# Two attention stages of a decoder step put into one fixed order of 328 ticks

## What is computed

```python
def stick_breaking_block(q, k, v, bias, q_pos, k_pos):
    z = jnp.einsum('bqhd,bkhd->bhqk', q.astype(jnp.float32), k.astype(jnp.float32)) * (HEAD_DIM ** -0.5)
    z = z + bias.astype(jnp.float32)[None, :, None, None]
    causal = k_pos[None, :] < q_pos[:, None]
    log_1m_beta = jnp.where(causal, jax.nn.log_sigmoid(-z), 0.0)
    tail = lax.cumsum(log_1m_beta, axis=3, reverse=True) - log_1m_beta
    w = jnp.where(causal, jnp.exp(jax.nn.log_sigmoid(z) + tail), 0.0)
    return jnp.einsum('bhqk,bkhd->bqhd', w.astype(v.dtype), v)
...
            k_past = cache_k[l][page_table].reshape(n_seq_s, past_len, N_HEADS_A, HEAD_DIM)
            v_past = cache_v[l][page_table].reshape(n_seq_s, past_len, N_HEADS_A, HEAD_DIM)
```

## Time and profile before

| | |
|---|---|
| median of 3 runs | 3228.53 us (3222.68 to 3229.23) |
| profiled execution, time / span | 3214.24 us / 3212.8 us |
| granted TensorE clock, mean | 0.942 of 2.4 GHz |
| prompt attention | from 728.4 us on |
| sample attention | from 1295.8 us on |
| router phase | from 1736.3 us on |

### The profile page before, as it was taken

One profiled execution on the slowest core, in us unless ns is written; L12 is line 12 of the kernel. 1 busy time (PEld: TensorE's weight loads), 2 busy tenths in 40 slices (PEclk: granted clock), 3 DMA queues, 4 the chain that ended last, 5 costly groups with the idle time before them and its releaser, 6 DMA issues. The chain is left out here.

```text
span 3212.8 us, 46045 instructions
## 1 busy us (share of the span) xinstructions
PE 2718.3 (85%) x15013; PEld 1382.8 (43%) x15013; DVE 1392.2 (43%) x2495; ACT 936.0 (29%) x1751; POOL 543.6 (17%) x695
## 2 busy tenths in 40 slices
PE   7999999977888888687876999859999999899950
PEld 3444444423444444444432444425555554455520
DVE  3141423228999999233322677622222221122137
ACT  2313030217888888222221221110100110000014
POOL 0101010100000000233331333311111111111136
PEclk9999999988999999799987999879999999999975
DMA  7020101066132500799996333367697669968637
GB/s 294 13 79 26 66 26 40 27 258 210 43 121 84 167 11 1 237 356 341 325 341 189 117 119 118 112 228 246 234 312 241 213 204 328 359 221 276 219 110 253
DMA packets 275565, 575.30 MB, mean 179 GB/s; under 512 B 59210, under 2 KB 75659, under 8 KB 271168
## 3 DMA queue, kind: packets, MB, share of 16 engines
q1 hardware_dynamic: 192620, 427.99, 38.3%
q0 software_dynamic: 82480, 145.43, 14.0%
q10 hardware_dynamic: 324, 0.10, 0.0%
HBM read 460.86 MB, written 112.29 MB: 178 GB/s over the span
## 5 line engine op out<-in xcount | busy, mean ns | idle before, releaser
L1936 PE MATMUL h<-w,xT 128*64 128x256 f32 x5120 | 588.9, 383 | 15.4 <-DMA w<-in_w 14.1
L1936 PEld LDWEIGHTS h<-w,xT 128*64 128x64 f32 x5120 | 362.3, 138 | 237.6 <-issue 67.6
L968 DVE TENSOR_TENSOR_SCAN left<-leave,left 128x512 f32<-128x512 f32 (+3 forms) x320 | 357.6, 1118 | 26.5 <-ACT leave L931 26.3
L418 PE MATMUL bank<-xnT,w_in 128*128 128x512 f32 x768 | 330.3, 592 | 0.0
L1949 PE MATMUL yb<-w,hT 128*64 128x512 f32 x1280 | 309.9, 605 | 0.0
L1010 PE MATMUL tb<-ident,w 128*128 128x128 f32 x1088 | 177.1, 287 | 87.2 <-DVE w L959 85.4
L1917 ACT ACTIVATE sg<-h 128x128 f32<-128x128 f32 x160 | 44.3, 277 | 684.9 <-PE h L1936 684.9
L1598 PE MATMUL pb<-w_out,featT 128*128 128x512 f32 x512 | 227.2, 597 | 2.0 <-DVE t L1663 2.0
L418 PEld LDWEIGHTS bank<-xnT,w_in 128*128 128x128 f32 x768 | 145.6, 190 | 181.8 <-issue 180.8
L418 PE MATMUL bank<-w_in,xnT 128*128 128x512 f32 x512 | 220.4, 592 | 0.0
L931 ACT ACTIVATE leave<-zb,nbiasP 128x512 f32<-128x512 f32 (+3 forms) x320 | 207.9, 650 | 40.7 <-DVE w L959 27.1
(11 more groups left out here) (366 smaller groups left out, 2947.3 us busy)
## 6 DMA issues: line engine op xcount, KB each, us to landing
w<-in_w SPq DMA_DIRECT2D x96, 2048.0 KB, 20.1
vp<-in_cache_v POOLq DMA_DIRECT2D x256, 256.0 KB, 4.9
w<-in_cache_k SPq DMA_DIRECT2D x256, 256.0 KB, 4.8
ys_d<-zeros SPq DMA_DIRECT2D x32, 816.0 KB
slab<-in_w_ada SPq DMA_DIRECT2D x24, 1024.0 KB, 18.2
ys_d<-y POOLq DMA_DIRECT2D x83, 256.0 KB, 9.8
x_in<-xs_d POOLq DMA_DIRECT2D x162, 128.0 KB, 6.2
w_in<-in_w_in SPq DMA_DIRECT2D x5, 2048.0 KB, 21.0
```

Source lines behind the costliest of these rows:

```text
L418: mm = pe.matmul(ps[:, :], w, m, start=(i == 0), stop=(i == len(parts) - 1))
L968: dve.tensor_tensor_scan(left[n % 4][:, at:at + cols][:, ::-1], leave[n % 4][:, 0:cols][:, ::-1], leave[n % 4][:, 0:cols][:, ::-1], left[n ...
L1936: mm = pe.matmul(h[half][q * G:q * G + G, 0:2 * P], xT[:, c % (XW // P), c // (XW // P) * G:c // (XW // P) * G + G], w13[i][:, c, :, cols] ...
```

## The change

The two phases become one, `attention_phase`, written out over 328 ticks (`TICKS`), and every engine follows the same list. Tick n holds the prompt's step n as before. From tick 3 on, each 19 ticks (`WINDOW`) also hold one sample unit (`place` gives unit and position p in it): at p = 0 to 15 one of its sixteen key transposes (`k_turn`), at p = 17 its scores, at p = 18 its scan, and in the window behind it at p = 2 its turned weights (`w_turn`) and at p = 5 and 13 the two halves of its product with the values.

What PE turns, and the scores of the samples too, goes by turns to two banks `tb` (`EVENTS`, `bank`): PE may write event e when event e-2 has been copied out (`free`). Before, prompt turns had three banks, and the samples' keys, scores and weights four, one and one. The copy of step n's weights now comes at tick n+3 instead of n+4. DVE copies every fourth prompt turn and the key turns at p = 3, 7 and 11; ACT copies all others, 13 of a unit's 16 key turns and the weights. The product is written over `take` (no `w`), so ACT's sigmoids also wait for the turn four steps back. `left` holds only one group of keys, so each step gets a new small instruction on DVE that writes its last column (`first`: a memset on the diagonal, 128 times, else a copy of one column, 192 times).

Keys have two page buffers instead of four, values two instead of four; key pages stand in SP's queue with the zero pieces, two of them in each unit. `rowsS` and `rowsP` serve as `kTs`, and are therefore loaded later, by POOL at the start of the router phase, where DVE waits for them. The new tokens' weights take one matmul with a widened operand instead of four.

```diff
-    LAG = 4
+    PPC = 4
+    CH = PPC * PAGE
+    NY = PAST // CH
+    NU = 2 * NY
+    FIRST, WINDOW, TICKS = 3, 19, N + 8
+
+    def place(n):
+
+        return divmod(n - FIRST, WINDOW) if n >= FIRST else (-1, 0)
+
+    EVENTS = []
+    for n in range(TICKS):
+        unit, p = place(n)
+        if 2 <= n < N + 2:
+            EVENTS.append((("turn", n - 2), "dve" if (n - 2) % 4 == 0 else "act"))
+        if p == 0 and unit in (1, NY + 1):
+            EVENTS.append((("new_turn", unit // NY), "dve"))
+        if p == 0 and unit in (NY + 1, NU + 1):
+            EVENTS.append((("out", unit // NY - 1), "dve"))
+        if p == 2 and 1 <= unit <= NU:
+            EVENTS.append((("w_turn", unit - 1), "act"))
+        if p < 4 * FC and 0 <= unit < NU:
+            EVENTS.append((("k_turn", unit, p), "dve" if p in (3, 7, 11) else "act"))
+        if p == 16 and unit in (0, NY):
+            EVENTS.append((("new_scores", unit // NY), "act"))
+        if p == 17 and 0 <= unit < NU:
+            EVENTS.append((("scores", unit), "act"))
+    EVENT = {name: e for e, (name, _) in enumerate(EVENTS)}
...
-        tb = [k.ps(f"tb{i}", [P, GRP]) for i in range(3)]
+        tb = [k.ps(f"tb{i}", [P, GRP]) for i in range(2)]
         ob = k.ps("ob", [P, 2, 2 * P])
-        s_set, s_one, s_z, s_lv, s_tk, s_sc, s_w, s_t, s_cd, s_ca, s_pv, s_o, s_fill, s_rows = (
-            k.sem(f"p4_{n}") for n in ("set", "one", "z", "lv", "tk", "sc", "w", "t", "cd", "ca", "pv", "o", "fill", "rows"))
...
+        def turned(eng, *name):
+
+            eng.wait_ge(s_t, EVENT[name] + 1)
+
+        def copied(eng, *name):
+
+            e = EVENT[name]
+            engine = EVENTS[e][1]
+            eng.wait_ge(s_ca if engine == "act" else s_cd, sum(other == engine for _, other in EVENTS[:e + 1]))
+
+        def bank(*name):
+
+            return tb[EVENT[name] % 2]
+
+        def page(eng, which, dst, sem, u, j):
+
+            first = (4 * (u // NY) + j) * NPAGES + (NY - 1 - u % NY) * PPC
+            for i in range(PPC):
+                number = eng.value_load(pages[0:1, first + i:first + i + 1], min_val=0, max_val=NPHYS - 1)
+                eng.dma_start(dst[:, i, :], cache[which][ds(number, 1)].rearrange("a p n -> (a p) n")).then_inc(sem, 16)
 
...
+                sp.wait_ge(s_pg, 16)
+                for u in range(NU):
+                    for j in range(4):
+                        g = 4 * u + j
+                        if g >= 2:
+                            turned(sp, "k_turn", (g - 2) // 4, 4 * ((g - 2) % 4) + FC - 1)
+                        page(sp, "cache_k", kp[g % 2], s_kp[g % 2], u, j)
+                        if g == 1:
+                            new_rows(0)
+                            load(1)
+                            sp.wait_ge(s_set, 1)
+                        if j == 1:
+                            zero_rows(2 * u)
+                        if j == 3:
+                            zero_rows(2 * u + 1)
+                            if u == 2:
+                                new_rows(1)
+                            if u in (4, 8):
+                                load(u // 4 + 1)
...
+                pool.wait_ge(s_pg, 16)
+                for u in range(NU):
+                    for half in range(2):
+                        if u or half:
+                            pool.wait_ge(s_spv, 2 * u + half)
+                        for i in range(2):
+                            page(pool, "cache_v", vp[i], s_vp[i], u, 2 * half + i)
...
+                for n in range(TICKS + 1):
+                    if n < N:
+                        pair, _, _, par, cols = item(n)
+                        head = 2 * pair + par
+                        act.wait_ge(s_z, n + 1)
+                        if n >= 4:
+                            act.wait_ge(s_sc, n - 3)
+                            turned(act, "turn", n - 4)
+                        act.activation(leave[n % 4][:, 0:cols], zb[n % 4][:, 0:cols], ACT.Sigmoid, scale=-SCALE,
+                                       bias=keep["nbiasP"][:, head:head + 1]).then_inc(s_lv, 1)
+                        act.activation(take[n % 4][:, 0:cols], zb[n % 4][:, 0:cols], ACT.Sigmoid, scale=SCALE,
+                                       bias=keep["biasP"][:, head:head + 1]).then_inc(s_tk, 1)
+                    if 0 <= n - 3 < N and (n - 3) % 4:
+                        turn(n - 3)
+                    u, p = place(n - 1)
+                    if p == 2 and 1 <= u <= NU:
+                        w_turn(u - 1)
+                    if p < 4 * FC and p not in (3, 7, 11) and 0 <= u < NU:
+                        k_turn(u, p)
...
+                def first(n):
+
+                    _, t, c, _, cols = item(n)
+                    if n >= 4:
+                        dve.wait_ge(s_w, n - 3)
+                    if c == t // TPG:
+                        dve.memset(left[n % 4][:, cols:cols + 1], 1.0).then_inc(s_in, 1)
+                    else:
+                        dve.tensor_copy(left[n % 4][:, GRP:], left[n % 4][:, 0:1]).then_inc(s_in, 1)
...
+                def scan(u):
+                    if u:
+                        dve.wait_ge(s_sw, u)
+                    dve.tensor_copy(s_left[:, CH:], s_left[:, 0:1])
+                    dve.drain()
+                    copied(dve, "scores", u)
+                    dve.tensor_tensor_scan(s_left[:, 0:CH][:, ::-1], s_leave[:, ::-1], s_leave[:, ::-1], s_left[:, CH:],
+                                           ALU.mult, ALU.bypass)
+                    dve.drain()
+                    dve.tensor_tensor(s_take[:, :], s_take[:, :], s_left[:, 1:], ALU.mult).then_inc(s_sw, 1)
...
+                def free(*name):
+
+                    e = EVENT[name]
+                    if e >= 2:
+                        copied(pe, *EVENTS[e - 2][0])
+                    return bank(*name)
...
+                def k_turn(u, p):
+                    j, f = p // FC, p % FC
+                    g = 4 * u + j
+                    if f == 0:
+                        pe.wait_ge(s_kp[g % 2], 64 * (g // 2) + 64)
+                    to = free("k_turn", u, p)
+                    for i in range(PPC):
+                        mm = pe.transpose(to[:, i * P:i * P + P], kp[g % 2][:, i, f * P:f * P + P], ident[:, :])
+                    mm.then_inc(s_t, 1)
...
+                for n in range(TICKS):
+                    m, q = n // 4, n % 4
+                    if m + 1 < M and q % 2:
+                        scores(m + 1, q // 2)
+                    if 2 <= n < N + 2:
+                        turn(n - 2)
+                    u, p = place(n)
+                    if p == 0 and u in (1, NY + 1):
+                        new_turn(u // NY)
+                    if p == 0 and u in (NY + 1, NU + 1):
+                        out(u // NY - 1)
+                    if p == 2 and 1 <= u <= NU:
+                        w_turn(u - 1)
+                    if p < 4 * FC and 0 <= u < NU:
+                        k_turn(u, p)
+                    if p == 16 and u in (0, NY):
+                        new_scores(u // NY)
+                    if p == 17 and 0 <= u < NU:
+                        sample_scores(u)
+                    if q == 0 and 2 <= m < M + 2:
+                        values(m - 2)
+                    if p == 3 and u in (1, NY + 1):
+                        new_values(u // NY)
+                    if p == 5 and 1 <= u <= NU:
+                        sample_values(u - 1, 0)
+                    if p == 13 and 1 <= u <= NU:
+                        sample_values(u - 1, 1)
...
+                pool.dma_start(keep["rowsS"][:, :, :], io["mod_d"][1:, :].unsqueeze(1).to_broadcast([BS, TS, 4 * D])).then_inc(s["rows"], 16)
+                pool.dma_start(keep["rowsP"][:, :, :], io["mod_d"][0:1, :].to_broadcast([P, 4 * D])).then_inc(s["rows"], 16)
...
+                dve.wait_ge(s["rows"], 32)
```

611 lines of the change are left out of this document (231 added, 380 removed).

## The result

| | before | after |
|---|---|---|
| median of 5 runs each | 3227.27 us | 3207.02 us (3194.1 to 3211.14) |
| ratio, 95% interval | | 0.9934 [0.9914, 0.9953] |
| profiled execution, time / span | 3214.24 / 3212.8 us | 3194.1 / 3192.6 us |
| attention, one or both stages | 1007.6 us | 980.8 us |

The account below looks back on a forecast made before the run. PE was to bound the merged stage: 777 us of work, 79 of waiting and 25 of ends make 881 against 1007.6; with router +5, 122 us less, 3092, plus 14.3 carried along: 3107 us, range 3010 to 3185.

Parts of the forecast that it names:

- What bounds, and how much work there is: Merged attention stage: PE becomes the longest engine with 777 us of work, DVE 633, ACT about 615, DMA 607.
- the term of 315 at full clock: Sample units' work on PE in the merged stage: 325 us from bursts over 16 units, taken as 315 at full clock.
- What the fixed order adds: Waiting of PE in the merged stage caused by the one written order of ticks: 79 us in sum, the softest term.
- The walk through one item: One four-step prompt item in the merged stage takes 10.3 us against 7.7 before, with PE waiting 1.6 to 1.8 us.
- Ends: Start and end of the merged stage: first scores 7.5 us, first key pages 3, end 10, last ticks 5; sum 25.
- Pages: Key and value page loads in the merged stage stay hidden, by 2 and 3 us; nothing charged.
- Router: Router start: loading `rowsP` and `rowsS` there delays the first `w_out` load by 0 to 8 us, taken as 5.
- PE packs better: Rival: a PE that never waits hides matmul fills; stage 785 to 825, kernel 3010 to 3050 us; 0.22, with fewer waits.
- DVE stays the bound: Rival: DVE's work and waits set the merged stage at 720 us, kernel 2945; 0.06 for DVE-bound or otherwise below 3010.
- Pages come late: Rival: late key and value loads add 86 us to the stage, kernel 3193; within the 0.17 for late pages or more waiting.
- Slower by SP's queue: Rival: zero pieces ahead of key groups in SP's queue make the stage 1044 us, kernel 3270; chance 0.08 for slower.
- late pages or more waiting: Outcome class for the kernel's time, 3140 to 3222 us, from late page loads or more waits; chance 0.17.

## Why the prediction was wrong

The stage was 100 us longer than forecast: 69 us are idle PE, 31 are PE's busy time.

**What bounds, and how much work there is: right, but for the clock.** PE is the longest engine, DVE and ACT came out within 2%, and cuts of PE's work came back nearly or wholly (78 us gave 71, 81 gave 80, in the profiled executions). PE's busy time was 808 against 777. The 777 hold the prompt stage as it ran before, of which 6 us are the cost of the lower clock, and the samples' work "at full clock": 770 us with the lower clock taken out. The changed kernel has 769.6. So the work was right, and the step that failed is the term of 315 at full clock, with "its clock near 1.0": at 13 of the 16 units' scans, where PE stops, a stretch at the lower clock begins. All such stretches cost 38 us, the 16 of them after 800 us cost 31. The Trainium skill (Perfetto Trace Analysis, "Identifying the Most-Contended Engine") warns that TensorE's busy time is no measure of how near it is to its limit; these runs agree, with 20 us between two banks and three for the same 5194 matmuls after the clock is taken out. How the third bank saves them no run here shows.

**What the fixed order adds: this is the larger step that failed.** The walk through one item was nearly right. What I took off afterwards was not. The 104 us of idle PE were 173; counted by place, with the means of the table above:

| term | predicted | in the trace |
|---|---|---|
| ordinary waits, 80 items | 118 (1.5 each) | 141 (1.76 each) |
| caught up in 32 value blocks | -32 | -28 (0.88 against 1.76) |
| caught up in 16 score blocks, and ticks with no key turn | -16 - 15 | 1 (1.83 against 1.76) |
| a unit's scan and product, and the sigmoids | 16 + 8 | 30 (3.61 against 1.76) |
| start of the stage | 7.5 + 3 | 7.9 + 5.8 + 7.7 |
| end, and what is left | 15 | 8 |
| sum | 104 | 173 |

(The last measured number is what the others leave of 173.) First, the 31 us taken off at the units' scores are not there: a stretch with a score block and fewer key turns waits as long as one without. Off an ordinary 1.5 us of waits a unit I had taken 1.9. Second, the ordinary waits were 0.3 us an item too low, 23 us. Third, the stop of DVE at a unit's scan was rightly placed and only a little too small, 24 against 30 us, but I did not see how it works: DVE's copy, for which PE waits, stands behind one or two scans and products in DVE's row, so that single waits reach 4.6 us. Nor did I expect a lower clock behind such a stop. Moving these copies ahead of the scan as well as the product took 26 us off the time with the product first, and moving them to ACT took 56 off the changed kernel's, with nothing else changed. In the stage the new order of DVE's row (product and copies) saved 34 us of idle PE and 14 of busy time, of which 12 are the clock's.

**Two banks: right in kind.** The runs give the third bank 52 us, DVE's order 51, the router's rows 6 to 14. Together they give 102 to 108, so the bank and the order are causes of their own that overlap by some 10 us, about what two medians leave uncertain; neither needs the other.

**Ends: half.** First scores as predicted. Then PE did not wait for the first key pages, where I had 3 us, but 5.8 for DVE, which waited for `s_bias`: I had looked through the queue for what PE needs and not for what stands early in DVE's row. And it waited 7.7 for the third key group. The first wait covers one for key pages, as the run with the small loads late shows: without `s_bias` PE waits 6.4 us for the first key group, and the start hardly gains.

**Pages: right.** Charged at nothing, and loading no pages gave 8 us with overlapping intervals; there is no value wait and, after the third group, one key wait of 3.0 us (at 1035.96) and two below 1. The third group is the rival of SP's queue in small: a zero piece ahead of it, once in the stage instead of in each window. As to an issue beside a busy DVE: POOL's 256 issues took 0.537 us in the mean with 192 one-column copies on DVE, as the 0.54 of the earlier trace rows. 36 of them overlap such a copy in time, and they took 0.5370 us in the mean, the 220 others 0.5366. The rule of the Trainium skill (SBUF — State Buffer, "SBUF: two separate sides") on a shared port, as the prediction read it, would have lengthened these 36; the trace does not show it for copies of one column.

**Router: 5 predicted, 6.8 measured.**

**Rivals.** "PE packs better" and "DVE stays the bound" are out for the changed kernel. "Pages come late" gave 3193, near the measured time, by a mechanism that the run without pages excludes. "Slower by SP's queue" occurred once, for 7.7 us. (Its threshold was off by the router's 5 us, which come off 1007.6 and were added: the stage breaks even at 1003 us, not 1012.) I had only "late pages or more waiting" above 3140, with 0.17; the waiting was the likelier half of it.

**Where I was wrong by my own signs.** PE busy 82% of the stage instead of 88; granted clock 0.95 instead of near 1.0; one key wait above a microsecond after the first unit. The sign "the waits are ended by ACT's and DVE's copies, a bank's" held. DVE ended 81 of 170 us of PE's waits, ACT 66 and DMA 24, so "DVE ends most" was close but not met.

## What to carry to other kernels

When two stages are merged into rows written out in one order, walk the rows of the engines that serve the bound one, not only the bound one's: work that it waits for must stand ahead of instructions that wait themselves (here products and copies ahead of scans, 51 us), and a rare extra instruction costs what stands between it and the next thing wanted. Do not take more off for catching up than there are waits to take it from. Charge the clock too: where the bound engine is TensorE, a stop can be paid twice, once as idle time and once in the work behind it at a lower clock (here 38 us over the stage). And compare like with like: waits near an event include those that would have been there without it. Look in every engine's row for a wait for a load that only the other stage needs.

## What was not expected of the hardware

The granted clock fell for short stretches in the middle of a stage in which PE is busy 82% of the time: 20 stretches at 0.50, 16 of them after 800 us and 13 of these at a unit's scan, cost 38 us of PE's time (4.35 us of work in the 8.2 us ahead of 872.40). Before, the prompt stage had a mean of 0.98. The same 5194 matmuls took PE 808, 792 and 770 us of busy time in three kernels; of the first 16 us of difference 15 are the clock's, and the next 22 came with the third bank, at an equal clock. In the first 18 us of the stage, in which PE worked 4.45 us, the clock granted was 0.59, between its two levels of 1.2 and 2.4 GHz, and the first scores took 1.65 us for what takes 0.9 later (64x384).
